# Local means of the pooling branch: shifted adds on VectorE and GpSimd in place of band matmuls, in a hybrid encoder layer

## The reference

```python
POOL_WINDOWS = (2, 4, 8, 16)
def multiscale_pool(u, w_grp, scale):        # u: (B, S, 1024)
    ...
    for g, w in enumerate(POOL_WINDOWS):
        lo = np.clip(t - w // 2, 0, S)
        hi = np.clip(t + w // 2, 0, S)
        win_sum = jnp.take(csg, hi, axis=1) - jnp.take(csg, lo, axis=1)
        mean = win_sum / jnp.asarray(hi - lo, jnp.float32)[None, :, None]
        outs.append(mean - uf[:, :, g])
    p = jnp.einsum('bsgc,gcd->bsgd', p, w_grp).reshape(B, S, D_POOL)
    return p * scale

def encoder_layer(x, c, ...):
    mod = jnp.einsum('bd,de->be', jax.nn.silu(c), ada_w) + ada_b
    shift, scale, gate = jnp.split(mod, 3, axis=-1)
    h = rms_norm(x, g_pre) * (1.0 + scale) + shift
    u_pool, q, k, v, z = jnp.split(h @ w_in, ...)
    y_pool = multiscale_pool(u_pool, pool_w, pool_scale)
    y_ret = bidir_retention(q, k, v, dec_f, dec_b)   # chunks of 128 tokens, 8 heads
    y = jnp.concatenate([y_pool, y_ret], axis=-1) * jax.nn.silu(z)
    return x + gate * rms_norm(y @ w_out, g_post)
```

## Time and profile before

| | us |
|---|---|
| median of 3 runs | 3200.8 (3198.46 to 3683.71) |
| profiled execution | 3200.19 |
| span of its slowest core, number 3 | 3198.4 |
| TensorE busy in the span | 3012.1 (94%) |
| VectorE busy | 2212.1 (69%) |
| ScalarE busy | 1258.1 (39%) |
| GpSimd busy | 1148.8 (36%) |

### The profile page before, as it was taken

The page is one execution under the profiler, slowest core; times in us unless marked ns, Lnnn a source line. Parts: engine busy times, 40 slices in busy tenths (PEclk is TensorE's granted clock), DMA queues, the critical chain, the costliest instruction groups (busy, mean ns, idle before and its releaser), DMA issues.

```text
span 3198.4 us, 51337 instructions; the slowest of 8 cores (3188.4 to 3198.4 us)
## 1 busy us (share of the span) xinstructions
PE 3012.1 (94%) x18160; PEld 1530.4 (48%) x18160; DVE 2212.1 (69%) x2510; ACT 1258.1 (39%) x1995; POOL 1148.8 (36%) x1007
## 2 busy tenths in 40 slices
PE   0699999999999999999979999999999999999997
PEld 0344444444444444444435555555555555555553
DVE  5557666666666566666357787778777877787774
ACT  3444433334344343443223444444444443444442
POOL 1433343334333232323113434444444443444443
PEclk9899999999999999999989999999999999999999
DMA  7855665456756665554677777777778777877774
GB/s 151 206 154 143 174 159 153 141 153 164 184 157 174 161 174 144 162 145 127 207 188 198 221 204 198 209 221 204 204 205 226 204 205 202 230 204 205 200 204 130
DMA packets 508200, 583.34 MB, mean 182 GB/s; under 512 B 328614, under 2 KB 353190, under 8 KB 500012
## 3 DMA queue, kind: packets, MB, share of 16 engines
q1 hardware_dynamic: 503340, 554.88, 62.7%
q0 software_dynamic: 4032, 20.97, 4.5%
q10 hardware_dynamic: 576, 4.19, 0.4%
HBM read 307.80 MB, written 202.91 MB: 160 GB/s over the span
## 4 chain that ended last, share of the span: by engine, by line
PE 88%; DVE 4%; DMA 4%; issue 2%; ACT 1%; POOL 0%; SPq 0%; DVEq 0%; POOLq 0%; ACTq 0%
PE psum L839 58%; PE psum L1349 21%; PE psum L1282 4%; DVE hT L827 2%; PE psum L992 1%; PE psum L1239 1%; PE psum L1315 1%; PE psum L935 1%; DMA yT<-yr 1%; DMA xn<-x 1%; DMA ypS<-yo 1%; PE psum L1055 1%; DMA xn<-wv 1%; DVE psum L905 0%; DMA QT<-qo 0%
## 5 line engine op out<-in xcount | busy, mean ns | idle before, releaser
L1289 POOL TENSOR_TENSOR rs<-st,mhalf 128x8 f32<-128x8 f32 x96 | 158.7, 1653 | 832.7 <-DVE st L1288 832.7
L839 PE MATMUL psum<-wu,hT 128*128 128x512 bf16 x1536 | 358.5, 388 | 39.8 <-DVE hT L827 37.3
L1349 PE MATMUL psum<-wo,yp 128*128 128x512 bf16 x1536 | 366.2, 382 | 15.0 <-DMA yT<-yr 14.9
L911 POOL TENSOR_TENSOR kb<-kr,kd 128x1024 bf16<-128x1024 bf16 x94 | 178.7, 1901 | 539.2 <-DVE kr L906 539.2
L1349 PE MATMUL psum<-wo,yT 128*128 128x512 bf16 x1536 | 364.7, 380 | 0.0
L904 DVE TENSOR_TENSOR t<-psum,rn 128x1024 f32<-128x1024 f32 x96 | 117.5, 1224 | 351.9 <-PE psum L839 346.7
L839 PE MATMUL psum<-hT,wq 128*128 128x512 bf16 x1536 | 349.7, 381 | 6.4 <-DVE yo L999 6.4
L839 PE MATMUL psum<-wzr,hT 128*128 128x512 bf16 x1536 | 349.6, 381 | 1.3 <-ACT SF L1319 1.3
L839 PE MATMUL psum<-hT,wzp 128*128 128x512 bf16 x1536 | 347.2, 379 | 0.0
L839 PE MATMUL psum<-wv,hT 128*128 128x512 bf16 x1472 | 332.7, 379 | 0.0
L839 PE MATMUL psum<-wk,hT 128*128 128x512 bf16 x1472 | 332.7, 379 | 0.0
(11 more groups left out here) (180 smaller groups left out, 4864.7 us busy)
## 6 DMA issues: line engine op xcount, KB each, us to landing
xn<-x SPq DMA_DIRECT2D x192, 512.0 KB, 5.2
y<-xn SPq DMA_DIRECT2D x96, 512.0 KB, 2.7
hS<-hT SPq DMA_DIRECT2D x24, 1024.0 KB, 5.6
krS<-kr SPq DMA_DIRECT2D x96, 256.0 KB, 2.0
vS<-vA SPq DMA_DIRECT2D x96, 256.0 KB, 5.7
ypS<-yo SPq DMA_DIRECT2D x24, 1024.0 KB, 8.5
hT<-hS SPq DMA_DIRECT2D x24, 1024.0 KB, 7.3
QT<-qo SPq DMA_DIRECT2D x384, 64.0 KB, 2.5
```

Source lines behind the costliest of these rows:

```text
L839: last = e.matmul(pp(p, half * 512, half * 512 + 512), lhs(half, dc), rhs(half, dc), start=(dc == 0), stop=(dc == 7))
L911: pool(lambda e: e.tensor_tensor(out=h3(kb[:, :]), in0=h3(kr[:, :]), in1=bch(kd[:, 1, :]), op=ALU.mult), 2.3, r=[krb, kdb_], w=[kbb])
L1289: pool(lambda e: e.tensor_tensor(out=rs[:, :], in0=st[:, :], in1=mhalf[:, :], op=ALU.pow), 1.65, r=[stb, mhalfb], w=[rsb])
L1349: last = e.matmul(pp(p, half * 512, half * 512 + 512), l_, wo[:, ec, half * 512:half * 512 + 512], start=(ec == 0), stop=(ec == 15))
```

## The change

u is now made with channels on the partitions and tokens in the row: the matmul's operands are swapped, a tile holds 256 channels (window j) of a group's 512 tokens in f32, with a halo of 8 columns on each side. Small copies fill the halos between neighbouring groups. The window's sum is made by shifted adds along the row, each doubling the width (two adds for window 4, three for 8, four for 16); the first add of windows 8 and 16 is on GpSimd, all others are on VectorE. One more instruction scales by 1/w and subtracts the token, and the product with the gate reads SBUF in place of PSUM. At the ends of a sequence a short product with `edge` corrects the divisor. The band tables and the band matmuls are gone; u tiles are six of 4.1 KB in place of ten of 2 KB, xh has three buffers in place of four.

The output gate's row is made in pass A in eight pieces of 128 columns: a load of f32 columns with conversion (GpSimd's queue), eight matmuls, two short VectorE instructions, a store. The conversion of `adag` in memory, its four loads between the passes and `gate_row` are gone. All u stages, the last group's too, stand in pass A's loop.

```diff
-    for j, w_ in enumerate(POOL_W):
...
+    dve(lambda e: e.memset(edge[:, :, 0, :], 1.0), 0.1, a=[edgeb])
+    for j in range(1, 4):
...
-    def stage_u(s, c, ht, hb):
-        i = c % 4
+    def stage_u(s, g, j):
+        ht, hb, _ = hTile[(s, g)]
         p = sc.pair("pu")
-        mm16(p, lambda half, dc: ht[:, dc, i * 128:(i + 1) * 128], lambda half, dc: wu[:, dc, half * 512:half * 512 + 512], [hb, wub])
+        mm16(p, lambda half, dc: wu[:, dc, (2 * j + half) * 128:(2 * j + half + 1) * 128], lambda half, dc: ht[:, dc, :], [hb, wub])
         u, ub, _ = u_r.next()
-        act(lambda e: e.copy(out=u[:, :], in_=pp(p)), 1.05, r=[p], w=[ub])
+        act(lambda e: e.copy(out=u[:, :, 8:8 + G], in_=pp(p).rearrange("p (b t) -> p b t", b=2)), 1.05, r=[p], w=[ub])
+        if g == NG[s] - 1:
+            dve(lambda e: e.memset(u[:, :, 8 + G:UW], 0.0), 0.1, r=[ub], a=[ub])
+        else:
+            n, nb = uT_[(s, g + 1, j)]
+            dve(lambda e: e.tensor_copy(out=u[:, :, 8 + G:UW], in_=n[:, :, 8:16]), 0.1, r=[nb, ub], a=[ub])
+            dve(lambda e: e.tensor_copy(out=n[:, :, 0:8], in_=u[:, :, G:8 + G]), 0.1, r=[nb, ub], a=[nb])
...
-    def stage_band(s, g, j, sz, szb):
...
+    def stage_pool(s, g, j, sz, szb):
+        u, ub = uT_.pop((s, g, j))
+        w_ = POOL_W[j]
+        tok = lambda t: t[:, :, 8:8 + G]
+        if j == 0:
+            m, mb, _ = s_r.next()
+            dve(lambda e: e.tensor_tensor(out=tok(m), in0=u[:, :, 7:7 + G], in1=tok(u), op=ALU.subtract), 1.15, r=[ub], w=[mb])
+        else:
+            a_, ab_, _ = s_r.next()
+            (pool if j > 1 else dve)(lambda e, a_=a_: e.tensor_tensor(out=a_[:, :, 1:UW], in0=u[:, :, 0:UW - 1], in1=u[:, :, 1:UW], op=ALU.add),
+                                     2.1 if j > 1 else 1.15, r=[ub], w=[ab_])
+            for l in range(1, j + 1):
+                d_ = 1 << (l - 1)
+                b_, bb_, _ = s_r.next()
+                lo_, hi_ = 2 * d_, UW - 2 * d_ + (1 if l == 1 else 0)
+                dve(lambda e, a_=a_, b_=b_, d_=d_, lo_=lo_, hi_=hi_: e.tensor_tensor(
+                    out=b_[:, :, lo_:hi_], in0=a_[:, :, lo_ - d_:hi_ - d_], in1=a_[:, :, lo_ + d_:hi_ + d_], op=ALU.add), 1.15,
+                    r=[ab_], w=[bb_])
+                a_, ab_ = b_, bb_
...
+            m, mb, _ = s_r.next()
+            dve(lambda e, a_=a_: e.scalar_tensor_tensor(out=tok(m), in0=tok(a_), scalar=1.0 / w_, in1=tok(u), op0=ALU.mult, op1=ALU.subtract),
+                1.15, r=[ab_, ub], w=[mb])
...
+        def gate(e):
+            if j:
+                return e.tensor_tensor(out=yo[:, :, 2 * j:2 * j + 2, :].rearrange("p c b t -> p b c t"), in0=v4(tok(m)),
+                                       in1=sz[:, :].rearrange("p (b c t) -> p b c t", b=2, c=4), op=ALU.mult)
...
+    def gate_cols(fc, after):
...
+            op("pe", f, mmc(8, 128), r=[b, scTb], w=[p])
...
+            if slot >= 6 and gfc < 8 and slot % 2 == 0:
+                gate_next = gate_cols(gfc, pace)
+                gfc += 1
```

More of the change, by code:

```diff
@@ L29 @@
 NPAIR = 4
-BW = 144
+UW = G + 16
 LAST = {}
@@ L761, in build_program @@
+    dve(lambda e: e.reciprocal(out=edge[:, :, 1:4, :],
+                               in_=edge[:, :, 1:4, :]), 0.4, r=[edgeb], w=[edgeb])
     pmod = sc.pair("pmod")
@@ L998, in stage_band @@
         yo, yob, yk = yoT[0]
[L999 to L1002, removed]
+        v4 = lambda t: t.rearrange("p b (c t) -> p b c t", c=4)
+        def gate(e):
+            if j:
+                return e.tensor_tensor(out=yo[:, :, 2 * j:2 * j + 2, :].rearrange("p c b t -> p b c t"), in0=v4(tok(m)),
+                                       in1=sz[:, :].rearrange("p (b c t) -> p b c t", b=2, c=4), op=ALU.mult)
+            last = None
+            for b in range(2):
+                last = e.scalar_tensor_tensor(out=yo[:, :, b, :], in0=m[:, b, 8:8 + G].rearrange("p (c t) -> p c t", c=4), scalar=0.5,
+                                              in1=sz[:, b * G:(b + 1) * G].rearrange("p (c t) -> p c t", c=4), op0=ALU.mult, op1=ALU.mult)
+            return last
+        dve(gate, 1.2, r=[mb, szb], **({"w": [yob]} if j == 0 else {"a": [yob]}))
         if j == 3:
@@ L1092, in build_program, with f, out @@
     dma(rTS.ap()[0], fl(rT[:, :, :]), "rT", r=[rTb], w=[dbuf("rTS", 0)], after=[wzp_d])
-    for c in cs0:
-        stage_u(s0, c, ht, hb)
+    for j in range(4):
+        stage_u(s0, g0, j)
+    def gate_cols(fc, after):
+        t, b, nm = ag_r.next()
+        g_, gb_, gk_ = gs_r.next()
+        dma(fl(t[:, :, :]), adagd.ap()[fc], nm, w=[b], q="pool", after=after)
+        dma(g_[0:2, 0:2, :].rearrange("p a b -> p (a b)"), growd.ap()[fc], gk_, w=[gb_], after=after)
+        p = sc.pair("pg")
+        def f(e):
+            last = None
+            for dc in range(8):
+                base = (p.phys or 0) * 1024
+                last = e.matmul(psum[0:2, base:base + 128], scT[:, dc, :], t[:, dc, :], start=(dc == 0), stop=(dc == 7))
+            return last
+        def out():
+            op("pe", f, mmc(8, 128), r=[b, scTb], w=[p])
+            p2 = lambda: psum[0:2, (p.phys or 0) * 1024:(p.phys or 0) * 1024 + 128]
+            dve(lambda e: e.tensor_tensor(out=g_[0:2, 2, :], in0=p2(), in1=g_[0:2, 0, :], op=ALU.add), 0.2, r=[p, gb_], a=[gb_])
+            dve(lambda e: e.scalar_tensor_tensor(out=g_[0:2, 2, :], in0=g_[0:2, 2, :], scalar=float(D) ** 0.5, in1=g_[0:2, 1, :],
+                                                 op0=ALU.mult, op1=ALU.mult), 0.2, r=[gb_], w=[gb_])
+            dma(ggS.ap()[:, fc * 128:(fc + 1) * 128], g_[0:2, 2, :], "ggst", r=[gb_], a=[dbuf("ggS")])
+        return out
     conv = []
-    for nm, src, dst, n_ in (("wqS", wqd, wqS, 8), ("wzrS", wzrd, wzrS, 8), ("woutS", woutd, woutS, 16), ("adagS", adagd, adagS, 8)):
+    for nm, src, dst, n_ in (("wqS", wqd, wqS, 8), ("wzrS", wzrd, wzrS, 8), ("woutS", woutd, woutS, 16)):
         for i in range(0, n_, 2):
@@ L1105, in build_program @@
     tgen = 1
+    gate_next, gfc = None, 0
     for k in range(1, len(groupsA)):
@@ L1121, in build_program @@
             pend_kv = (s, c, kb, kbb, v, vb)
-            if j == 0 and k + 1 == len(groupsA) and ps == s:
-                stage_u(s, c, ht, hb)
-            stage_band(ps, pg, j, sz, szb)
+            stage_pool(ps, pg, j, sz, szb)
+            if gate_next is not None:
+                gate_next()
+                gate_next = None
             pace = [o for o in sc.ops[-60:] if o.q == "pe"][-1:]
@@ L1149, in build_program @@
         ci += 1
+    if gate_next is not None:
+        gate_next()
+    while gfc < 8:
+        gate_cols(gfc, ())()
+        gfc += 1
     while tgen < NG0:
@@ L1397, in build_program @@
     ht, hb, _ = hTile[(ps, pg)]
[L1398 to L1405 removed]
     for j in range(4):
         sz, szb = stage_zp(ps, pg, j)
[L1408 to L1412 removed]
+        stage_pool(ps, pg, j, sz, szb)
+        if j > 1:
+            stage_q(0, j - 2)
+    stage_q(0, 2)
     q3 = stage_q(0, 3)
```

111 lines of the change are left out of this document (35 added, 76 removed).

## The result

| | before | after |
|---|---|---|
| median of 3 runs | 3200.8 us | 3326.9 us |
| profiled execution | 3200.2 | 3326.9 |
| start, to pass A's first u matmul in the loop | 165.6 | 167.9 |
| loop of pass A, to the start of its last v stage | 1399.8 | 1540.3 |
| a group of four slots (the loop holds 22.93) | 61.05 | 67.2 |

The change makes the kernel slower: ratio 1.0394, 95% interval 1.0349 to 1.0439. The loop loses 140.5 us, the passage between the passes gives back 26.2, the start loses 2 and pass B 10. Three u stages of the last group (3 x 3.45 us) stood behind the last v stage before and are in the loop now; a full group of four slots took 61.5 us before.

The account below looks back on a forecast made before the run. TensorE bounds pass A now; after the change VectorE and its collisions with GpSimd would set the group's pace. From 3200 us, +84 (loop) and -8 (start) give 3275 us, range 3125 to 3360.

Parts of the forecast that it names:

- The loop: Pass A: a group of four slots goes from 61.5 to 65.3 us, +84 us for 22 full groups.
- The band: Pass A, TensorE: removing the band matmuls saves 0.57 us per slot, 2.3 us per group.
- the second rival: Pass A: waits at group starts lower TensorE's clock, adding 2.8 us a group, 3337 us in all; chance 0.12.
- The gate row's pieces: Pass A: eight matmuls, eight times, cost TensorE some 4 us in all, covered by its new idle time.
- The collisions: Pass A: seven of eight long GpSimd multiplications (1.90 us each) per group hit VectorE's two-SBUF-operand instructions; a quarter of small work collides.
- The first rival: Pass A: collisions fall into VectorE's waits and TensorE stays the bound; without any collision 3122 us; chance 0.22.
- The two adds ahead of the affine step: Fourth slot: they delay the next group's affine step to 62.3 us against TensorE's 57.6; TensorE stands still about 5 us.
- Busy shares: Pass A's profile: VectorE over 90% busy, TensorE waiting for hT over 100 us in all.
- The start: Before the loop: without band tables the first norm's scale and shift start 12 us earlier; taken as -8 us (0 to -15).
- Between the passes: Gate row and u stages leave, about 18 us of VectorE work stays: 0 us, with -15 to +15.
- Pass B: Second pass: not touched by the change, no term in the sum.
- The lock in full: Third rival: every GpSimd instruction reading SBUF blocks VectorE, 73 us a group, 3450 us; chance 0.04.

Follow-up runs that it names:

- e3: Changed kernel with GpSimd scaling one head of eight in kb and SB, the other heads' scaling left out: ratio 0.997 to the kernel before, 61.6 us a group.
- e2: Changed kernel with both GpSimd multiplications (kb and SB) done by ScalarE, eight activations each: no ratio, 3163.1 us profiled, 59.7 us a group.
- e1: Changed kernel with window 16's shifted adds in each group's fourth slot waiting until the affine step is done: ratio 1.022 to the kernel before.
- e9: Changed kernel with kb and SB on ScalarE in the loop, affine step before the adds, and a fourth xh buffer in the start: ratio 0.978 to the kernel before.
- e4: Kernel before with only the output gate's row moved into pass A in eight pieces: ratio 0.988, interval 0.971 to 1.005.
- e8: Kernel before, band matmuls kept, with kb and SB on ScalarE in the loop, gate row in pass A and last u stages in the loop: ratio 0.990.
- e5: Changed kernel with kb and SB scaled by ScalarE in pass A's loop and the affine step ahead of window 16's adds: ratio 0.984 to the kernel before.
- e7: Kernel before, band matmuls and gate row unchanged, with kb and SB scaled by ScalarE in pass A's loop: ratio 0.992 to the kernel before.

## Why the prediction was right, and where not

The forecast was 3275 us, range 3125 to 3360; the time is 3326.9, slower by 3.9%. The mechanism held, and its sum was too small by 52 us. By its steps:

- **The loop.** Forecast 61.5 to 65.3 us a group, +84 us for 22 groups; measured 61.5 to 67.2, +140.5 for the loop. TensorE's standing still, 5 us a group plus 3.0 not laid out, came to 171 us in 22 waits, 7.8 each: right in size. The band was too: 0.57 us a slot forecast, 0.60 measured. What the sum lacked is three terms. The clock, which the forecast left at full speed and the second rival priced at 2.8 us a group, costs 2.0 (46.4 us at 23 starts), 34 us more than before. The last group's three u stages, which the prediction itself moves into the loop, add 10 us there and stand in no sum. The gate row's pieces, put under idle time, add 5.
- **The collisions.** Seven of eight were laid out by hand at 1.6 to 1.9 us, 12.4 us a group, and 1.5 for the small work; the trace has 11.7 in all. e3, where the two multiplications are cut to an eighth, gains 5.6 us a group; e2 7.5, part of it order. The first rival, that the collisions fall into waits, did not hold: a group is above its 61.5 us.
- **The two adds ahead of the affine step.** Shown by e1: about 2 us a group. The difference of e2 and e3 is as large, but part of it can be the work that e3 leaves on GpSimd.
- **Busy shares.** VectorE was to be over 90% busy; it is at 87%. The in-order wait of the halo copies for ScalarE's u copy, 56 us of the stretch or 3.1 a group, wasn't in the layout. Since the collisions were laid out some 2 us a group too long, the right size of TensorE's waits is in part luck. The adds alone have 1.21 to 1.25 us with maxima of 2.75, as said. That affine steps keep 3.5 us holds where GpSimd's work meets them (3.52 at one place, 3.29 at another), not everywhere (1.87).
- **The start.** Forecast -8, measured +2: the step that failed. "The xh ring loses a buffer; its tiles live under two slots, so nothing" holds in the changed kernel's loop. In the start the fourth chunk waits 24.1 us for the first transpose, and behind it stand ScalarE's tables, then VectorE's. What the band tables freed, this took. e9 shows it: 16 us.
- **Between the passes.** Forecast 0 within 15, measured -26.2: outside, and past the 15 us that the prediction named as a sign of being wrong. 10.4 of it are the three u stages that went to the loop. With the gate row alone the passage falls by 13.3 us (e4), and from e8 to e5, band against adds, by 7.9. It also falls by 8.2 us from before to e7, where the passage was left as it is, so the parts can't be told apart to better than that.
- **Pass B.** Said to be untouched; it loses 10 us, in its first hundred: in the 110 us from its first scores TensorE is busy 97 us, 103 before. Most of it is one wait. VectorE's product of the first scores (scm) stands behind a rope of q that waits 5.4 us for TensorE, and TensorE then waits 6.7 us for scm; before, scm starts at 1645.96 us, 1.9 us behind the first scores, and there is no such wait. All eight kernels with shifted adds have this wait of 6.7 us and take 1556 to 1565 us from the first scores on; the four with the band don't have it and take 1549 to 1554. No run altered that order, so the wait is shown and its cause is argued. VectorE and TensorE of the kernel after (start us, us):

```profile
1771.06 1.22 DVE L1216 TENSOR_TENSOR t<-psum,rT 128x1024 f32<-128x1024 f32 x1 [5.43 <-PE psum L825]
...
1776.07 1.22 DVE L1280 TENSOR_TENSOR scm<-psum,dtot 128x1024 bf16<-128x1024 f32 x1
...
1777.65 0.27 PE L1319 MATMUL psum<-vB,scm 128*128 128x128 bf16 x1 [6.70 <-DVE scm L1280]
```

Start, passage and pass B together gave 14 us where the forecast gave 8, so the error of the sum lies in the loop. The lock in full, 73 us a group if everything met, did not come: 67.2. The Trainium skill, "SBUF — State Buffer", section "Who interferes with whom", says that whoever comes second is blocked until the first is done. The trace agrees in the fourth slot shown, in both directions: kb takes 2.90 us there (2.77 in the median of the stretch) where 1.90 is its length alone. The same page and section of the Trainium skill say that a VectorE instruction with at most one SBUF input outside its two-port modes doesn't contend with GpSimd. The trace agrees: rope's last instruction (one PSUM operand) lies between 1.224 and 1.226 us in all 70 cases.

## What to carry to other kernels

The move of work from TensorE to VectorE was priced here by what GpSimd does beside it, not by VectorE's free time: look which GpSimd instruction the moved ones release or meet, and try that one on ScalarE first. When instructions are added ahead of a step that the critical engine waits for, count them with their collisions, and put the step first. A ring that loses a buffer is checked at the start as well, where loads, transposes and tables run at once.

## What the runs showed of the hardware

- GpSimd's kb multiplication is lengthened by VectorE as VectorE is by it: 1894 ns at least, 2767 in the median of 70. A GpSimd instruction on one element, ssq's, takes 834 ns in the mean beside VectorE's work and 336 in e2.
- A shifted add of 1024 to 1054 elements takes 0.71 us in the median in bf16 against 1.25 in f32, operands one column apart included; the scalar_tensor_tensor instruction of 1024 elements takes 1.2 us in either type.
- Eight activations of 128 elements with a scale per partition take ScalarE 0.39 us each and 2.44 us together, where GpSimd takes 1.9 us for the whole and holds VectorE up.
